# Retention: values and gates token by row in one product per head, gate ahead of the output's transposes, output product by token halves

## The reference, cut to what matters

```python
h = rmsnorm(x, g)
q, k, v, gate = split(h @ w_in_a)              # 8 x 128, 8 x 128, 8 x 256, 8 x 256
scores = (q k^T) * decay_mask                  # inside a chunk of tokens
inter  = (q * q_decay) @ state                 # from earlier chunks
state  = state * chunk_decay + (k * k_decay)^T v
o = scores @ v + inter
o = (o - mean(o)) * rsqrt(var(o) + EPS)        # per token and head, over 256
y = o * silu(gate)
x = x + rmsnorm(y @ w_out_a, g2)               # w_out_a: 2048 x 1024
```

## Time and profile before

| what | value |
| --- | --- |
| median of 3 runs | 2768.59 us (2767.56 to 13394.39) |
| the profiled execution's own time | 2768.7 us |
| its span, first to last instruction | 2767.0 us |
| PE busy | 2705.5 us, 98% of the span |
| DVE busy | 1625.5 us, 59% |
| ACT busy | 717.1 us, 26% |
| POOL busy | 328.9 us, 12% |
| mean granted PE clock | 0.993 of full speed |
| chain that ended last | PE 92%, DVE 4%, POOL 2%, DMA 1% |

### The profile page before, as it was taken

One profiled execution on the slowest core, in us unless ns is written; L12 is line 12 of the kernel. 1 busy time (PEld: TensorE's weight loads), 2 busy tenths in 40 slices (PEclk: granted clock), 3 DMA queues, 4 the chain that ended last, 5 costly groups with the idle time before them and its releaser, 6 DMA issues.

```text
span 2767.0 us, 35646 instructions
## 1 busy us (share of the span) xinstructions
PE 2705.5 (98%) x13436; PEld 2187.0 (79%) x13452; DVE 1625.5 (59%) x2058; ACT 717.1 (26%) x1319; POOL 328.9 (12%) x310
## 2 busy tenths in 40 slices
PE   9899989999999999999999999999999999999987
PEld 7667757888888888878888888888886888888766
DVE  8856563764545555565454454454476666666665
ACT  5333341421111111132021021021034444444441
POOL 0899900000000000021000000000000000000000
PEclk9999999999999999999999999999999999999999
DMA  5211113253434343424222222222243222222214
GB/s 191 76 62 61 61 46 114 100 186 143 157 121 152 122 166 129 166 84 168 90 78 76 91 76 76 91 76 76 91 152 122 77 76 76 76 76 78 74 63 166
DMA packets 50891, 287.66 MB, mean 104 GB/s; under 512 B 6800, under 2 KB 7952, under 8 KB 20880
## 3 DMA queue, kind: packets, MB, share of 16 engines
q1 hardware_dynamic: 23072, 119.92, 12.6%
q0 software_dynamic: 14544, 105.91, 11.2%
q10 hardware_dynamic: 13216, 61.02, 5.8%
HBM read 249.08 MB, written 29.36 MB: 101 GB/s over the span
## 4 chain that ended last, share of the span: by engine, by line
PE 92%; DVE 4%; POOL 2%; DMA 1%; issue 1%; ACT 0%; SPq 0%; DVEq 0%; POOLq 0%; ACTq 0%
PE OBB L243 11%; PE OBB L244 11%; PE OBB L245 11%; PE PB L243 11%; PE PB L245 11%; PE PB L244 11%; PE TBB L1000 4%; PE TBB L243 3%; PE TBB L245 3%; PE TBB L244 3%; PE PB L1049 2%; PE OBB L1114 2%; PE PB L1055 1%; PE OBB L1109 1%; PE PB L2216 1%; PE PB L2218 1%
## 5 line engine op out<-in xcount | busy, mean ns | idle before, releaser
L243 PE MATMUL PB<-HH,WH 128*128 128x512 f32 x1296 | 513.6, 396 | 4.2 <-DVE HL L405 3.0
L245 PE MATMUL PB<-HH,WL 128*128 128x512 f32 x1296 | 504.7, 389 | 0.0
L244 PE MATMUL PB<-HL,WH 128*128 128x512 f32 x1296 | 504.4, 389 | 0.0
L243 PE MATMUL OBB<-HH,WH 128*128 128x512 f32 x1120 | 454.8, 406 | 8.7 <-DVE WL L259 5.7
L244 PE MATMUL OBB<-HL,WH 128*128 128x512 f32 x1120 | 439.8, 393 | 0.0
L245 PE MATMUL OBB<-HH,WL 128*128 128x512 f32 x1120 | 439.4, 392 | 0.0
L243 PEld LDWEIGHTS PB<-HH,WH 128*128 128x128 f32 x1296 | 243.3, 188 | 61.0 <-issue 5.2
L244 PEld LDWEIGHTS PB<-HL,WH 128*128 128x128 f32 x1296 | 243.3, 188 | 54.6 <-issue 4.8
L245 PEld LDWEIGHTS PB<-HH,WL 128*128 128x128 f32 x1296 | 243.2, 188 | 51.1
L259 DVE TENSOR_TENSOR WL<-RAW,WH 128x2048 fp32r<-128x2048 f32 x101 | 234.1, 2318 | 61.6 <-DMA WH<-units 59.8
L2760 POOL DMA_DIRECT2D WH<-units x85 | 46.1, 542 | 1818.9 <-PE PB L243 891.9
(11 more groups left out here) (394 smaller groups left out, 4168.2 us busy)
## 6 DMA issues: line engine op xcount, KB each, us to landing
WH<-units POOLq DMA_DIRECT2D x85, 1024.0 KB, 5.1
RAW<-units SPq DMA_DIRECT2D x85, 1024.0 KB, 4.7
gs<-units ACTq DMA_DIRECT2D x16, 1024.0 KB, 4.8
gu<-gs ACTq DMA_DIRECT2D x16, 1024.0 KB, 3.9
RAW<-gu SPq DMA_DIRECT2D x16, 1024.0 KB, 5.0
WH<-gu POOLq DMA_DIRECT2D x16, 1024.0 KB, 5.5
tmpd<-xr SPq DMA_DIRECT2D x112, 64.0 KB, 2.0
A<-xT SPq DMA_DIRECT2D x8, 512.0 KB, 8.6
```

Source lines behind the costliest of these rows:

```text
L243: first = pe.e.matmul(out, wh, xh, start=start, stop=False)
L244: pe.e.matmul(out, wh, xl, start=False, stop=False)
L245: return pe.e.matmul(out, wl, xh, start=False, stop=stop), first
```

## The change

- The weights of values and gates are laid out anew in the two units `u0+1` and `u0+2`: each holds four of the eight k tiles, and for each k tile 512 columns, 256 of values and 256 of gates. A `block(b, slot, part)` takes the activations of 128 tokens as the stationary operand and these 512 columns as the moving one: 12 products per part, 24 per block, 8 blocks per head. Tokens are then the rows at once. ACT takes each block out of its bank in two operations of 256 columns, values by Copy and gates by Silu, both scaled by `rtok`, the row norm per token (`rtok` is made once, by eight small products inside the q/k product of the first head). DVE's scaling of values and gates goes, and so do the 16 transposes of the values.
- DVE multiplies `on` by the gates in SBUF (1024 columns per half, `og`), before PE turns it. The transposes go to PB0; ACT (`high`) and DVE (`low`) split the turned product straight from PSUM.
- The output product runs by halves of the tokens in every head (`out_tile`, banks of 512 columns), and DVE adds each half tile to `A` on its own. The order on PE and DVE inside a head is new.
- The row norm has to be there earlier: PE waits for it after k tile 6 of the first q/k product.
- The end of the retention block uses the same order; four of its squares are made by ACT earlier.
- SP issues the swaps of q0 and k0 before the third load of the last block. In the first block POOL issues the loads of units 6 and 7 after 10 and 20 pieces of the convolution, not after 13 and 22.

```diff
@@ ret_pe
+            def between(k):
+                if k == 5:
+                    ffn_total_pe(pe)
+                if k == 6:
+                    pe.e.wait_ge(act_done, done_in("act", "norm_a", "root"))
+                    ...
+                    for b in range(NB):
+                        mm = pe.e.matmul(OB[0][:, b:b + 1], rbx[:, b * P:(b + 1) * P], mean1[:, 0:1],
+                                         start=True, stop=True)
+                    mm.then_inc(pe_done, pe.mark("rtok"))
...
+            def block(b, slot, part):
+                tokens = slice(b * P, (b + 1) * P)
+                for n in range(4):
+                    k, w = 4 * part + n, slice(n * HALF, (n + 1) * HALF)
+                    mm, first = mm3(pe, BLOCK_BANKS[b % 4][:, :], HH[:, k, tokens], HL[:, k, tokens],
+                                    WH[slot][:, w], WL[slot][:, w], k == 0, k == KT - 1)
...
             def body(i, u0):
-                slot = unit(pe, u0 + 1, i, 4)
+                a = unit(pe, u0 + 1, i, 4)
                 if i is not None:
-                    pe.e.wait_ge(dve_done, at_last(pe, "dve", f"y{KT - 1}", i))
-                dense(pe, OBB, slot, 0, HH, HL, "v0")
-                pe.e.wait_ge(dve_done, at_mark(pe, "dve", "qT", i))
-                dense(pe, PB[0], slot, 1, HH, HL, "v1")
+                    pe.e.wait_ge(dve_done, at_last(pe, "dve", f"y{KT - 1}_1", i))
+                for b in range(4):
+                    block(b, a, 0)
+                slot = unit(pe, u0 + 2, i, 4)
+                pe.fresh = False
+                for b in range(4):
+                    block(b, slot, 1)
                 pe.e.wait_ge(dve_done, at_mark(pe, "dve", "kT", i))
...
+                for b in (4, 5):
+                    pe.e.wait_ge(act_done, at_mark(pe, "act", f"g{b - 4}", i))
+                    block(b, a, 0)
+                pe.e.wait_ge(act_done, at_mark(pe, "act", "v3", i))
+                pe.e.wait_ge(act_done, at_mark(pe, "act", "kt1", i))
...
+                for b in (6, 7):
+                    pe.e.wait_ge(act_done, at_mark(pe, "act", f"g{b - 4}", i))
+                    block(b, a, 0)
+                outputs(0, i)
+                pe.fresh = True
+                for b in (4, 5, 6):
+                    block(b, slot, 1)
+                pe.e.wait_ge(act_done, at_mark(pe, "act", "v6", i))
                 pe.e.wait_ge(dve_done, at_mark(pe, "dve", "SM", i))
...
+                turned(0, i)
+                block(7, slot, 1)
+                outputs(1, i)
                 slot = unit(pe, u0 + 3, i, 4)
+                pe.e.wait_ge(dve_done, at_mark(pe, "dve", "yl1_0", i))
+                for m in range(6):
+                    out_tile(m, 0, slot, i)
+                turned(1, i)
+                for m in (6, 7):
+                    out_tile(m, 0, slot, i)
+                pe.e.wait_ge(dve_done, at_mark(pe, "dve", "yl1_1", i))
+                for m in range(KT):
+                    out_tile(m, 1, slot, i)
...
@@ ret_act
+            def block(b, i):
+                bank, scale = BLOCK_BANKS[b % 4], rtok[:, b:b + 1]
+                act.e.wait_ge(pe_done, at_mark(act, "pe", f"vg{b}", i))
+                e.activation(vr[:, b, :], bank[:, 0:256], ACT.Copy, scale=scale).then_inc(act_done, act.mark(f"v{b}"))
+                e.activation(gt[:, b, :], bank[:, 256:HALF], ACT.Silu, scale=scale).then_inc(
+                    act_done, act.mark(f"g{b}"))
...
@@ ret_dve
+                for j, x in enumerate("qk"):
+                    dve.e.wait_ge(pe_done, projected(dve, x, i))
+                    if j:
+                        low_part(dve, u0 + 2, i, 4)
...
+                states(0, 4, i)
+                variances(0, i)
+                normed(0, i)
                 low_part(dve, u0 + 3, i, 4)
+                states(4, 7, i)
+                low(0, i)
+                variances(1, i)
                 e.wait_ge(cleared, KT)
+                output(0, 0)
+                normed(1, i)
+                for m in range(1, 6):
+                    output(m, 0)
+                low(1, i)
+                for m in (6, 7):
+                    output(m, 0)
...
@@ block.gpsimd
-            for n, upto in ((5, 6), (6, 13), (7, 22), (8, 36), ...
+            for n, upto in ((5, 6), (6, 10), (7, 20), (8, 36), ...
@@ lay_out
-        two(n + 1, *(cols(w, 2048 + h * 256 + j * P) for j in range(2)))
-        two(n + 2, *(cols(w, 4096 + h * 256 + j * P) for j in range(2)))
+        vg = np.concatenate([w[:, 2048 + h * 256:2048 + (h + 1) * 256], w[:, 4096 + h * 256:4096 + (h + 1) * 256]], 1)
+        for j in range(2):
+            units[n + 1 + j] = rows(vg, j * 512, 512)
```

More of the change, by code:

```diff
@@ L510, in norm_a_act @@
             roots(act, TBB, rbx)
+            act.e.wait_ge(pe_done, done_in("pe", "ret_first", "rtok"))
+            act.e.activation(rtok[:, :], OB[0][:, 0:NB], ACT.Copy).then_inc(act_done, act.mark("rtok"))
         def xs_pieces():
@@ L2221, in body @@
-                gate(1, 0, slot, i)
-                for h in range(2):
-                    if h:
-                        gate(1, 1, slot, i)
-                    pe.e.wait_ge(dve_done, at_mark(pe, "dve", f"on{4 * h + 3}", i))
-                    for f in range(2):
-                        if h:
-                            pe.e.wait_ge(dve_done, at_mark(pe, "dve", f"yt{f}_0", i))
-                        transposes(pe, TB[f], lambda b: on[:, b, f * P:(f + 1) * P],
-                                   range(4 * h, 4 * h + 4), f"ot{f}_{h}")
@@ L2244, in ret_pe @@
+                if i is None:
+                    for m in range(4):
+                        total_second(pe, m)
             with pe.e.Fori(0, RET_HEADS - 1) as i:
@@ L2340, in ret_end_act @@
             e.preload_act_table_set(LN_EXP)
-            for m in range(KT):
+            for m in range(4, KT):
                 end_square_act(act, m, 0)
@@ L2390, in tile @@
                                 ALU.add).then_inc(dve_done, dve.mark(f"add{k}_{h}"))
-            for m in range(KT):
-                output(m, 0)
-                if m > 1:
-                    add_square(m - 1)
+            for m in range(1, KT - 1):
+                add_square(m)
             output(0, 1)
@@ L2509, in statistics, with normed @@
                     dve_done, dve.mark(f"var{h}"))
+            def normed(h, i):
+                bank, blocks = PB[h], slice(4 * h, 4 * h + 4)
                 dve.e.wait_ge(act_done, at_mark(dve, "act", f"root{h}", i))
@@ L2546, in body, with states @@
+            def states(first, after, i):
+                dve.e.wait_ge(pe_done, at_mark(dve, "pe", f"U{first // 4}", i))
+                for c in range(first, after):
                     u = PB[c // 4][:, (c % 4) * 256:(c % 4 + 1) * 256]
@@ L2720, in gained, with swaps @@
                      else io["gu"][bass.ds(m * 2 + u, 1)])
-            def swaps(i):
-                for x, h in FIRST if i is not None else (("q", 0), ("k", 0), ("q", 1), ("k", 1)):
+            def swaps(i, parts):
+                for x, h in parts:
                     sp.wait_ge(act_done, at_mark(steps, "act", f"raw{x}{h}", i))
@@ L2737, in _ @@
             sp.wait_ge(gain_out, 32 * DIFF_HEADS)
-            for n in range(3):
+            for n in range(2):
                 gained(U_DIFF + n, 0)
             steps.phase = "diff_first"
-            swaps(None)
+            swaps(None, (("q", 0), ("k", 0)))
+            gained(U_DIFF + 2, 0)
+            swaps(None, (("q", 1), ("k", 1)))
             steps.phase = "diff"
```

263 lines of the change are left out of this document (99 added, 164 removed).

## The result

The change made the kernel slower by a little: 2774.97 us median (10 runs) against 2767.81 (10 runs beside them), ratio 1.0029, 95% interval 1.0019 to 1.0038. One of the ten runs on each side was far slower (6738 and 13394 us), and the ratio leaves these two out. The profiled execution of the changed kernel has a time of 2774.2 and a span of 2772.5, 5.5 more than before. The forecast was 2774 by a sum of +5.4.

The account below looks back on a forecast made before the run. PE, densely busy, was taken to bound the retention loop. On the profiled 2768.7 us, 6.0 + 1.9 + 12.5 + 1.3 - 8.8 - 7.5 = +5.4 gave 2774 us; range for 8 in 10, 2757 to 2790.

Parts of the forecast that it names:

- Parts 1 to 4: Retention head: value transposes gone (-1.70), format changes, waits for ACT and DVE; +0.75 us a head, +6.0 for eight.
- Part 3: Retention head: PE waits for ACT's value copies of blocks 6 and 7, 0.8 us each, +1.6 a head.
- Part 4: Retention head, output tile 5: PE waits for DVE's add, 0.2 to 1.0 us, taken as +0.6 a head.
- part 2: Retention head: PE's changes of format between products and transposes cost 0.2 to 0.4 us, taken as +0.25 a head.
- copies free: Rival, retention loop: ACT and DVE keep ahead, so the waits for them cost nothing; 2756 us, chance 0.10.
- Part 5: First head's q/k product: eight small products for the row norm and their format changes cost +1.9 us, once.
- Part 6: First head: PE waits +9.5 us once for the third unit, loaded late by POOL; slowed clock adds +3.0.
- Part 7: End of the retention: DVE reaches the split of U_DIFF 20.2 us after the first output tile starts; +1.3 us.
- Part 8: Start of last block: earlier q0 and k0 swaps save -5.7 us of PE's wait and -3.1 of half clock.
- Part 9: First attention: earlier load of unit 6 saves -5.0 us of PE's wait and -2.5 of half clock.
- rival of a clock that falls in the loop: Retention loop: short waits send the clock to half, 3.1 us each; 2799 to 2849 us, chance 0.06.

Follow-up runs that it names:

- run 2: Changed kernel, but PE waits for ACT's copies of blocks 6 and 7 only at the products that read them: 2761.16 us, 0.9977 to before.
- run 1: Changed kernel, but POOL issues the first head's third-unit load ahead of its wait for stored activations and the memsets: 2766.67 us, 1.0002 to before.
- Run 7: Changed kernel, but before the last block ACT copies rotated q and k ahead of the second value half: 2772.26 us, 1.0019 to before.
- Run 10: The kernel of run 9, with DVE's two convolution taps of the first attention behind the split of unit 6: 2742.53 us, 0.9908 to before.
- run 11: The changed kernel itself, unchanged, measured once more: 2777.00 us, 1.0032 to before.
- run 9: Changed kernel with the edits of run 1, run 2 and Run 7, and DVE adding tile 1 before the gate product: 2748.23 us, 0.9927 to before.
- run 6: Kernel before, with only the change's convolution table and the q0 and k0 swaps ahead of the last block's third load: 2759.54 us, ratio 0.9973.

## Why the prediction was right where it was, and wrong where it was not

- *Parts 1 to 4, the head: +0.75 forecast, +0.36 measured, 2.9 and not 6.0 for eight.* Part 3 has the wait itself right, 0.80 at each place, and lacks the 0.10 behind it: the two cost 1.77 by run 2, not 1.6. Part 4 was mis-sized: 0.32, not 0.6, within its bounds of 0.2 to 1.0. With 1.70 less, and 1.77 and 0.32 more, nothing is left for the formats of part 2 (0.36 + 1.70 - 1.77 - 0.32 = -0.03), for which 0.25 was taken. The rival "copies free" fell for the reason given: the blocks rotate through four banks, as the Trainium skill, Perfetto Trace Analysis (Optimizing Tensor Performance, Matmuls), asks, and the reader right behind its own producer still lost 0.80. What frees it is not another bank but the order inside the group (run 2).
- *Part 5, `rtok`:* 1.9 forecast, 1.8 measured.
- *Part 6, the late unit:* 9.5 + 3.0 forecast, 11.3 measured, a wait of 8.5; this was the shortest of eight, the others are 9.0 to 9.8. The place and the reason are shown by run 1.
- *Part 7, the end of the retention:* +1.64 from head 8's transposes to U_DIFF, less head 8's own 0.36: 1.3, as forecast. DVE reaches the split of U_DIFF 20.9 us behind the first output tile (2072.55 - 2051.67), where 20.2 was worked out. The wait of 1.07 for DVE's last sum of squares was not foreseen.
- *Part 8, the swaps: -5.7 and -3.1 forecast, -3.8 and -1.5 measured.* The step that failed is "Behind its landing DVE has four operations, and PE is free at 2128.57 - 5.69 = 2122.9": it followed SP and DVE, but not ACT's queue, where the copy of q stands behind a value copy that itself waits for PE's last product. Run 7 shows it for the wait; what the clock does behind it stays open, since there it fell without a wait.
- *Part 9, the early load: -5.0 and -2.5 forecast, -4.7 and nothing (waits of 2.72 + 5.73 before, 3.84 now).* The step that failed is "DVE is free at 136.94 - 4.78 = 132.16", a time taken over from before: DVE was free at 133.33, and the split took 3.35. The moved load shifts POOL against DVE, DVE's tap grows by 1.4, and kT comes later. The clock falls in the longer wait for kT already, and the half clock is only moved: PE works 4.9 us under it in both kernels. Run 10 shows that DVE's queue held kT.
- *Not forecast:* -1.7 at 366, chance by run 11. Without it the two profiles would differ by 7.2, which is also what the medians differ by.

The costs came out 3.1 (heads), 1.2 (late unit) and 0.1 lower than forecast; of the savings 3.5 (swaps) and 2.8 (early load) were missing, and 1.7 came unforeseen. The errors cancel within 0.2. So the right sum is partly luck. The mechanisms of the costs are not: each wait was found where it was said to be. Of the two savings the first step of each is right, and what holds PE next was missed in both. The rival of a clock that falls in the loop is out: 24 short waits in heads of 103 us leave the granted clock at 1.00. The Trainium skill, TensorE: Matmul & The Clock Gate (A second HAM failure mode: psum-queue depth-cycling), describes that fall for another kernel; waits of 0.3 to 0.8 us did not bring it here.

## What to carry to other kernels

A semaphore wait belongs at the one instruction that needs it, not at the head of its group: two or six products in front of it hid 0.80 us twice a head, and a head became 1.77 us shorter. When a consumer is moved forward, look at where its load stands in the issuing queue, and when a wait is removed, follow every in-order queue that feeds the next one (here ACT's). Compare profiles place by place, since falls of the clock move a single execution by several us.

## What the runs showed of the hardware

- DVE and POOL in each other's way: POOL's two operations beside the tap take 1.05 and 1.27 us in the changed kernel, and DVE's tap 3.44; before, they take 1.37 and 2.25, and the tap 2.04. What one is spared the other pays. The Trainium skill, SBUF — State Buffer (SBUF: two separate sides), says that the pair of ports they share is locked for a whole instruction, by a DVE operation with two SBUF inputs or by POOL's, and that the loser stands still; both of these are such operations. The trace agrees that one of the two pays. That the loser stands still for the other's whole instruction it does not show: the tap lost 1.40 beside two operations of POOL of 2.27 together.
- The granted clock fell near 366 in 8 of 13 profiles, among them one of the two of the changed kernel itself, and each time it came to 1.6 or 1.7 us. The Trainium skill, TensorE: Matmul & The Clock Gate (What's actually happening), says that the same kernel gets different numbers of slow products at its start from run to run; the traces here show it in the middle of a kernel.
- It also fell where no wait was left (run 7), behind 16 products of one column and nine others, a stretch that the profile counts as busy; in run 9 it did not fall at this place.
- A swap of four DMAs of 64 KB took 5.7 to 6.3 us from issue to DVE's start with POOL's load beside them in ten profiles, and 8.1 in run 6's.
